# Dense gates of an encoder layer: part of one plane moves from VectorE to ScalarE, in four small instructions per eight tokens

## The chip, the cores and the metric

One core of one Trainium2 chip runs the whole kernel in one launch. TensorE (PE) multiplies matrices, VectorE (DVE) and ScalarE (ACT) do element-wise work, GpSimd (POOL) issues gathers, SyncE (SP) issues most other transfers. Each engine works through its own list of instructions in order; engines wait for one another by counting semaphores. The metric is the device time of one execution in microseconds (us). Before the change three runs gave 3988.33 us as the median, from 3973.1 to 3989.22.

## The reference, cut to what matters

The kernel computes one encoder layer for 1280 tokens: a token mixer (gated linear attention, a Fourier branch, gates), a layer norm, a mixture of 16384 experts of rank one (PEER), and a last norm. The part around the change is the expert mixture. For each token and each of 8 heads the 16 best pairs of keys are taken, so a token has 128 chosen experts with 128 softmax weights:

```python
s_top, i_top = lax.top_k(s, PEER_TOPK)                       # per head, two lists of 128 keys
cand = s_top[:, :, 0, :, None] + s_top[:, :, 1, None, :]
cand_idx = i_top[:, :, 0, :, None] * PEER_NKEYS + i_top[:, :, 1, None, :]
best, pos = lax.top_k(cand.reshape(t, PEER_HEADS, -1), PEER_TOPK)
idx = jnp.take_along_axis(cand_idx.reshape(t, PEER_HEADS, -1), pos, axis=-1)
g = jax.nn.softmax(best, axis=-1).reshape(t, PEER_HEADS * PEER_TOPK)
u = peer_u[idx]
a = jax.nn.gelu(jnp.einsum('td,ted->te', xb, u), approximate=False)
out = jnp.einsum('te,ted->td', g * a, peer_v[idx])
```

For 512 of the tokens the kernel gathers the rows of the chosen experts. For the other 768 it multiplies by all experts and needs, for each token, a table of 128 x 128 gates: entry (j, i) is the sum of the weights g of those of the token's 128 slots whose expert is 128 i + j. That table is what the stage "dense gates" makes.

## The kernel before

The stages follow one another, with a barrier of all engines between them: projection, attention, Fourier branch, merge, norm, best keys, best pairs, dense gates, experts. Only the function `dense_gates` (L1714 on) is changed.

Its 128 partitions are a token's 128 slots. On partition p, `R.i` and `R.j` hold for every token the two key numbers of the slot's expert, and `R.g_hi`, `R.g_lo` the slot's weight in two parts of 16 bits; `R.i`, `R.g_hi` and `R.g_lo` hold each value twice (TWICE = 2). VectorE works on eight tokens at a time (an octet, OCT = 8), in four instructions over 1024 elements of 16 bits per partition:

- L1780 compares the numbers 0 to 127 with the token's i: `hot_i`, one-hot over i (layout 64 pairs x 8 tokens x 2).
- L1783 does the same with j: `hot_j`, 128 x 8.
- L1786 multiplies `hot_i` by `g_hi`: `hot_g[:, s, 0]`, the plane of high parts.
- L1787 multiplies `hot_i` by `g_lo`: `hot_g[:, s, 1]`, the plane of low parts.

`hot_j` and `hot_g` have a ring of four octets (RING, s is the place in it); `hot_i` has one buffer. For each token TensorE multiplies `hot_j` (the weights that it loads) by the token's columns of the two planes, L1802 and L1803, and sums both in PSUM. Four tokens fill a bank (a quad); four banks are in use. ScalarE copies each quad to `out` (L1816, 512 elements), and SyncE stores half a body, 32 tokens, at a time (L1760, 2 MB). A body is 64 tokens: 8 octets, 16 quads. There are 12 bodies: the first is written out, eleven run in a loop.

What sets the order: TensorE waits at an octet's first quad for `hot_ok`, which VectorE raises with L1787, and for the bank four quads back to be copied out (`ev`). ScalarE waits for each quad (`mm`), and at every eighth quad for the store that last used that half of `out` (`stored`). VectorE waits before `hot_j` for TensorE to be done with the ring place of four octets ago (`mm`), before L1786 for its own `hot_i` (`i_ok`), and at the end of each octet for its own `hot_ok`, since the next octet overwrites `hot_i`. The stage ends when the last store has landed; only then do the expert stage's first loads start.

Of the kernel before, what the change touches and what calls it, by code (L numbers as in the profile page):

```python
# [25 lines left out]
f32 = mybir.dt.float32  # L26
f16 = mybir.dt.float16
u32 = mybir.dt.uint32
ALU = mybir.AluOpType
ACT = mybir.ActivationFunctionType  # L30
AX = mybir.AxisListType

P = 128
# [11 lines left out]
PH, NKEYS, TOPK, HALF = 8, 128, 16, 128  # L45
# [6 lines left out]
ND = DT * P  # L52
# [9 lines left out]
TWICE = 2  # L62
# [1640 lines left out]
I_GROUP = 4  # L1703
# [11 lines left out]
def dense_gates(nc, A, R):  # L1715

    with ExitStack() as c:
        sb = lambda n, s, d: c.enter_context(nc.sbuf_tensor(n, s, d))  # L1720
        sem = R.semaphore
        OCT, RING, HALF_T, QUAD = 8, 4, 32, 4
        PAIRED = NKEYS // TWICE
        BODY = 2 * HALF_T
        row = sb("g_row", [P, NKEYS], f32)
        iota, iota_2 = sb("g_iota", [P, NKEYS, OCT], f16), sb("g_iota_2", [P, PAIRED, OCT, TWICE], f16)
        hot_i, hot_j = sb("g_hot_i", [P, PAIRED, OCT, TWICE], f16), sb("g_hot_j", [P, RING, NKEYS, OCT], f16)
        hot_g = sb("g_hot_g", [P, RING, 2, PAIRED, OCT, TWICE], f16)
        out = sb("g_out", [P, 2, N_GROUPS, HALF_T, I_GROUP], f32)
        ps = c.enter_context(nc.psum_tensor("g_ps", [P, 4, QUAD, NKEYS], f32))  # L1730
        iota_ok, i_ok, hot_ok, mm, ev = [sem("g_" + n) for n in "iota_ok i_ok hot_ok mm ev".split()]
        stored = [sem("g_stored0"), sem("g_stored1")]
        h_in = sem("g_h_in")
        consts, consts_all = R.consts, R.consts_in + 16
        R.consts_in = consts_all
        block = c.enter_context(nc.Block())
        NQ, NO = BODY // QUAD, BODY // OCT
        TURNS = 1
        LOOP = (ND // BODY - 1) // TURNS
        REST = [n for n in range(1 + LOOP * TURNS, ND // BODY)]  # L1740

        def bodies(eng, body):
            body(0, 0, True)
            with eng.Fori(0, LOOP) as i:
                for r in range(TURNS):
                    body(1 + TURNS * i + r, 1 + r, False)
            for n in REST:
                body(n, n, False)

        @block.sync  # L1750
        def _(sp):
            sp.dma_start(row[:], A["iota"].rearrange("(a n) -> a n", a=1).to_broadcast([P, NKEYS])).then_inc(consts, 16)
            for tile in range(GT):
                sp.dma_start(h_rows(R, tile), R.h_dram[tile].rearrange("p (k c) -> p k c", k=KO)).then_inc(h_in, 16)

            with sp.Fori(0, ND // BODY) as i:
                for h in range(2):
                    sp.wait_ge(ev, NQ * i + NQ // 2 * (h + 1))
                    dst = R.g_dram[:, :, bass.ds(BODY * i + HALF_T * h, HALF_T)].rearrange("g j t f -> j g (t f)")
                    sp.dma_start(dst, out[:, h].rearrange("p g t f -> p g (t f)")).then_inc(stored[h], 16)  # L1760
            for h in range(2):
                sp.wait_ge(stored[h], 16 * (ND // BODY))
            sp.wait_ge(h_in, 16 * GT)

        @block.vector
        def _(dve):
            dve.wait_ge(consts, consts_all)
            for t in range(OCT):
                dve.tensor_copy(iota_2[:, :, t], row[:].rearrange("p (n c) -> p n c", c=TWICE))
            dve.tensor_copy(iota[:], row[:].rearrange("p (n a) -> p n a", a=1).to_broadcast([P, NKEYS, OCT])  # L1770
                            ).then_inc(iota_ok, 1)
            dve.wait_ge(iota_ok, 1)

            def body(n, turn, first):
                for o in range(NO):
                    s = (NO * turn + o) % RING
                    toks = bass.ds(BODY * n + OCT * o, OCT)
                    each = lambda ap: ap.rearrange("p (a t) c -> p a (t c)", a=1).to_broadcast([P, PAIRED, OCT * TWICE])
                    flat = lambda ap: ap.rearrange("p n t c -> p n (t c)")
                    dve.tensor_tensor(flat(hot_i[:]), flat(iota_2[:]), each(R.i[:, toks]), ALU.is_equal).then_inc(i_ok, 1)  # L1780
                    if not first or o >= RING:
                        dve.wait_ge(mm, 2 * (NO * n + o - RING + 1))
                    dve.tensor_tensor(hot_j[:, s], iota[:], R.j[:, toks].rearrange("p (a t) -> p a t", a=1).to_broadcast(  # L1783
                        [P, NKEYS, OCT]), ALU.is_equal)
                    dve.wait_ge(i_ok, NO * n + o + 1)
                    dve.tensor_tensor(flat(hot_g[:, s, 0]), flat(hot_i[:]), each(R.g_hi[:, toks]), ALU.mult)  # L1786
                    dve.tensor_tensor(flat(hot_g[:, s, 1]), flat(hot_i[:]), each(R.g_lo[:, toks]), ALU.mult).then_inc(hot_ok, 1)  # L1787
                    dve.wait_ge(hot_ok, NO * n + o + 1)
            bodies(dve, body)

        @block.tensor
        def _(pe):
            def body(n, turn, first):
                for q in range(NQ):
                    o, s = q // 2, (NO * turn + q // 2) % RING
                    if not first or q >= 4:
                        pe.wait_ge(ev, NQ * n + q - 3)
                    if q % 2 == 0:
                        pe.wait_ge(hot_ok, NO * n + o + 1)
                    for u in range(QUAD):  # L1800
                        t = QUAD * (q % 2) + u
                        pe.matmul(ps[:, q % 4, u], hot_j[:, s, :, t], hot_g[:, s, 0, :, t], start=True, stop=False)  # L1802
                        last = pe.matmul(ps[:, q % 4, u], hot_j[:, s, :, t], hot_g[:, s, 1, :, t], start=False, stop=True)  # L1803
                    last.then_inc(mm, 1)
            bodies(pe, body)

        @block.scalar
        def _(act):
            def body(n, turn, first):
                for q in range(NQ):  # L1810
                    h = q // (NQ // 2)
                    t0 = QUAD * (q % (NQ // 2))
                    if q % (NQ // 2) == 0 and not first:
                        act.wait_ge(stored[h], 16 * n)
                    act.wait_ge(mm, NQ * n + q + 1)
                    act.activation(out[:, h, :, t0:t0 + QUAD].rearrange("p g t f -> p t g f"),  # L1816
                                   ps[:, q % 4].rearrange("p t (g f) -> p t g f", f=I_GROUP), ACT.Copy).then_inc(ev, 1)

            bodies(act, body)

# [553 lines left out]
```

## Time and profile before

| | |
|---|---|
| median of three runs | 3988.33 us |
| the profiled execution | 3981.61 us, span of its instructions 3979.9 us |
| dense gates, first octet's start to last copy's start | 1555.6 to 1814.6 us |
| in 1555 to 1815 us: PE, DVE, ACT busy | 206.39, 240.43, 114.88 of 260 us |
| granted TensorE clock there | 0.50 |

The span is counted from the first instruction to the last. In a group of instructions "128x1024 f16" is partitions by elements and the type, "x96" the number of times, and the three durations are the shortest, the median and the longest. A row of the timeline has its start in us, its duration in us, engine, line, operation, and in brackets how long the engine had stood idle before it and what ended that. An instruction's duration can overlap the next one's start on the same engine, so the time that an instruction really takes from its engine is the distance between two starts. Matmuls are pipelined and overlap each other in the same way.

### The profile page before, as it was taken

The page shows a single profiled execution, that of the slowest core. Times are in us where ns is not written, and L with a number is a line of the kernel's source. Part 1 is how long each engine was busy: PE and PEld are TensorE (multiplying, and loading weights), DVE is VectorE, ACT ScalarE, POOL GpSimd, SP SyncE. Part 2 cuts the span into 40 slices and gives each one's busy share as a digit, 9 for nine tenths or more (in the row PEclk, how much of TensorE's full clock was granted, in tenths as well). Part 3 has the DMA queues.
Part 4 walks back from the last instruction along what each step waited for, and adds up shares of the span by engine and source line. Part 5 has one row for each costly group of instructions (what it writes and reads, how often), then busy time and mean ns, then how long its engine had stood idle before and what let it go on. Part 6 is the DMA issues. An engine that isn't in the chain of part 4 may idle for free. (4 is left out here: it accounts for less than half of the span.)

```text
span 3979.9 us, 59043 instructions
## 1 busy us (share of the span) xinstructions
PE 3521.8 (88%) x19562; PEld 1975.0 (50%) x19562; DVE 3010.2 (76%) x5573; ACT 1502.1 (38%) x2654; POOL 877.8 (22%) x943
## 2 busy tenths in 40 slices
PE   7988669996899386776899999999999999999995
PEld 3556535553455244674454545454545555454542
DVE  3444235555499798995888888888988898888888
ACT  3732233443233343443333333333333333333332
POOL 1210012220011010001233323332333333333323
PEclk9986589998899697557999999999999999999998
DMA  6740157873110102667889898999989898989885
GB/s 265 286 199 14 72 223 257 281 238 138 61 42 30 67 1 69 198 197 265 341 338 360 339 353 339 352 341 352 355 337 354 338 366 330 363 337 358 341 335 190
DMA packets 284839, 996.94 MB, mean 250 GB/s; under 512 B 21008, under 2 KB 124240, under 8 KB 217552
## 3 DMA queue, kind: packets, MB, share of 16 engines
q0 software_dynamic: 110592, 671.14, 45.0%
q1 hardware_dynamic: 174160, 324.66, 22.4%
q8 instruction: 52, 0.85, 0.1%
q14 instruction: 35, 0.29, 0.0%
HBM read 860.45 MB, written 135.27 MB: 250 GB/s over the span
## 5 line engine op out<-in xcount | busy, mean ns | idle before, releaser
L1949 POOL DMA_INDIRECT x_rows<-in_peer_uv,x_index x512 | 580.6, 1134 | 1083.4 <-DVE acc L2054 946.7
L128 PE MATMUL x_ps_v<-x_v,x_w_hi 128*128 128x512 f16 x1536 | 589.6, 384 | 82.3 <-DVE acc L2060 81.3
L2054 DVE SCALAR_TENSOR_TENSOR acc<-x_rows,x_share,acc 128x1024 f32<-128x1024 f32 x512 | 656.4, 1282 | 0.0
L2190 PE MATMUL x_ps_a<-h_hi,x_u_hi 128*128 128x256 f16 (+1 forms) x2048 | 621.2, 327 | 23.2 <-ACT x_u_hi L1965 16.0
L2191 PE MATMUL x_ps_a<-h_lo,x_u_hi 128*128 128x256 f16 (+1 forms) x2048 | 620.9, 327 | 0.0
L129 PE MATMUL x_ps_v<-x_v,x_w_hi 128*128 128x512 f16 x1536 | 589.2, 384 | 0.0
L130 PE MATMUL x_ps_v<-x_v,x_w_lo 128*128 128x512 f16 x1536 | 588.5, 383 | 0.0
L1985 ACT ACTIVATE x_dots<-x_dots 128x1 f32<-128x1 f32 x512 | 103.5, 202 | 976.0 <-DVE x_dots L2078 975.9
L2078 DVE CUSTOM_DVE_ANT_0 x_rows<-h_lo,x_rows 128x1024 f32<-128x1024 f32 x256 | 312.9, 1222 | 92.3 <-DMA x_rows<-in_peer_uv,x_index 91.4
L2195 PE MATMUL x_ps_a<-h_hi,x_u_lo 128*128 128x256 f16 (+1 forms) x2048 | 374.6, 326 | 0.0
L2078 DVE CUSTOM_DVE_ANT_0 x_rows<-h_hi,x_rows 128x1024 f32<-128x1024 f32 x256 | 312.6, 1221 | 23.3 <-DMA x_rows<-in_peer_uv,x_index 22.0
L128 PEld LDWEIGHTS x_ps_v<-x_v,x_w_hi 128*128 128x128 f16 x1536 | 151.6, 99 | 277.1 <-DVE acc L2060 97.5
L2190 PEld LDWEIGHTS x_ps_a<-h_hi,x_u_hi 128*128 128x128 f16 x2048 | 201.1, 98 | 161.5 <-ACT x_u_hi L1965 16.2
L2191 PEld LDWEIGHTS x_ps_a<-h_lo,x_u_hi 128*128 128x128 f16 x2048 | 201.0, 98 | 136.4 <-issue 1.1
L2195 PEld LDWEIGHTS x_ps_a<-h_hi,x_u_lo 128*128 128x128 f16 x2048 | 200.5, 98 | 132.3
L1802 PE MATMUL g_ps<-g_hot_g,g_hot_j 128*128 128x128 f16 x768 | 195.1, 306 | 60.2 <-DVE g_hot_g L1787 60.2
L2091 DVE TENSOR_TENSOR x_w<-x_w,x_gate 128x512 f32<-128x512 f32 (+1 forms) x256 | 142.2, 555 | 135.8 <-ACT x_w L1997 134.5
L130 PEld LDWEIGHTS x_ps_v<-x_v,x_w_lo 128*128 128x128 f16 x1536 | 151.7, 99 | 185.9 <-issue 7.9
L129 PEld LDWEIGHTS x_ps_v<-x_v,x_w_hi 128*128 128x128 f16 x1536 | 151.6, 99 | 177.9 <-issue 7.0
L2060 DVE SCALAR_TENSOR_TENSOR acc<-x_ps_v,acc 128x1024 f32<-128x1024 f32 x192 | 234.2, 1220 | 0.0
L1947 POOL COPY x_index<-expert 128x4 uint32 (+1 forms) x128 | 68.9, 538 | 639.2 <-DVE acc L2054 363.2
L1974 ACT ACTIVATE x_gate<-x_gate_st 128x1024 f32<-128x1024 f32 x96 | 200.1, 2084 | 11.1 <-DMA x_gate_st<-gate_scratch 8.0
(332 smaller groups left out, 6585.4 us busy)
## 6 DMA issues: line engine op xcount, KB each, us to landing
x_u_st<-in_peer_u_t SPq DMA_DIRECT2D x128, 512.0 KB, 7.0
x_v<-v_scratch SPq DMA_DIRECT2D x128, 512.0 KB, 9.8
gate_scratch<-g_out SPq DMA_DIRECT2D x24, 2048.0 KB, 8.7
x_gate_st<-gate_scratch SPq DMA_DIRECT2D x96, 512.0 KB, 6.6
m_v_st<-in_peer_v POOLq DMA_DIRECT2D x72, 512.0 KB, 5.6
v_scratch<-m_v_out POOLq DMA_DIRECT2D x72, 512.0 KB, 4.4
p_v_st<-in_peer_v POOLq DMA_DIRECT2D x46, 512.0 KB, 8.8
v_scratch<-p_v_out POOLq DMA_DIRECT2D x46, 512.0 KB, 7.4
```

Source lines behind the costliest of these rows:

```text
L128: pe.matmul(out, lhs_hi, rhs_hi, start=first, stop=False)
L129: pe.matmul(out, lhs_hi, rhs_lo, start=False, stop=False)
L130: return pe.matmul(out, lhs_lo, rhs_hi, start=False, stop=last)
L1802: pe.matmul(ps[:, q % 4, u], hot_j[:, s, :, t], hot_g[:, s, 0, :, t], start=True, stop=False)
L1949: pool.indirect_dma_start(rows[:, m % RING], None, uv_all, bass.IndirectOffsetOnAxis(ap=index[:, tile % 2, m % PER_TILE:m % PER_TILE + 1], ...
L1974: act.activation(gate[:, :, t0:t0 + PIECE], gate_st[:].rearrange("p t e -> p e t"), ACT.Copy).then_inc(gate_ok, 1)
L2054: dve.scalar_tensor_tensor(R.acc[:, DT + tile], rows[:, r, D:2 * D], share[:, s:s + 1], R.acc[:, DT + tile], ALU.mult, ALU.add).then_inc(v ...
L2060: dve.scalar_tensor_tensor(R.acc[:, t], ps_v[:, slot], 1 / (VSCALE * GSCALE), R.acc[:, t], ALU.mult, ALU.add).then_inc(added, 1)
L2078: dve.tensor_tensor_reduce(out=rows[:, k % RING, 0:D].rearrange("p (k c) -> p k c", k=KO), in0=h_rows(R, tile), in1=rows[:, k % RING, 0:D] ...
L2190: pe.matmul(out, u_hi[:, e, ko], R.h_hi[:, ko, t], start=ko == 0, stop=False)
L2191: pe.matmul(out, u_hi[:, e, ko], R.h_lo[:, ko, t], start=False, stop=False)
L2195: last = pe.matmul(out, u_lo[:, e, ko], R.h_hi[:, ko, t], start=False, stop=ko == KO - 1)
```

## The change

For tokens 4 to 7 of each octet the plane of low parts is made by ScalarE: one Copy per token of that token's 128 columns of `hot_i`, with the slot's `g_lo` as a scale per partition (function `lows`). [...] VectorE's product with `g_lo` covers tokens 0 to 3 only. `hot_i` gets two buffers, because ScalarE reads it while VectorE goes on. A new semaphore `low_ok` says that ScalarE is done with an octet: TensorE waits for it at the octet's second quad, and VectorE before it overwrites the `hot_i` of two octets ago.

```diff
--- before.py
+++ after.py
@@ -1724,11 +1724,13 @@
         BODY = 2 * HALF_T
         row = sb("g_row", [P, NKEYS], f32)
         iota, iota_2 = sb("g_iota", [P, NKEYS, OCT], f16), sb("g_iota_2", [P, PAIRED, OCT, TWICE], f16)
-        hot_i, hot_j = sb("g_hot_i", [P, PAIRED, OCT, TWICE], f16), sb("g_hot_j", [P, RING, NKEYS, OCT], f16)
+        hot_i, hot_j = sb("g_hot_i", [P, 2, PAIRED, OCT, TWICE], f16), sb("g_hot_j", [P, RING, NKEYS, OCT], f16)
         hot_g = sb("g_hot_g", [P, RING, 2, PAIRED, OCT, TWICE], f16)
+        low = sb("g_low", [P, ND], f32)
+        HALF_O = OCT // 2
         out = sb("g_out", [P, 2, N_GROUPS, HALF_T, I_GROUP], f32)
         ps = c.enter_context(nc.psum_tensor("g_ps", [P, 4, QUAD, NKEYS], f32))
-        iota_ok, i_ok, hot_ok, mm, ev = [sem("g_" + n) for n in "iota_ok i_ok hot_ok mm ev".split()]
+        iota_ok, i_ok, low_ok, hot_ok, mm, ev = [sem("g_" + n) for n in "iota_ok i_ok low_ok hot_ok mm ev".split()]
         stored = [sem("g_stored0"), sem("g_stored1")]
         h_in = sem("g_h_in")
         consts, consts_all = R.consts, R.consts_in + 16
@@ -1768,7 +1770,8 @@
             for t in range(OCT):
                 dve.tensor_copy(iota_2[:, :, t], row[:].rearrange("p (n c) -> p n c", c=TWICE))
             dve.tensor_copy(iota[:], row[:].rearrange("p (n a) -> p n a", a=1).to_broadcast([P, NKEYS, OCT])
-                            ).then_inc(iota_ok, 1)
+                            )
+            dve.tensor_copy(low[:], R.g_lo[:, :, 0]).then_inc(iota_ok, 1)
             dve.wait_ge(iota_ok, 1)
 
             def body(n, turn, first):
@@ -1777,14 +1780,21 @@
                     toks = bass.ds(BODY * n + OCT * o, OCT)
                     each = lambda ap: ap.rearrange("p (a t) c -> p a (t c)", a=1).to_broadcast([P, PAIRED, OCT * TWICE])
                     flat = lambda ap: ap.rearrange("p n t c -> p n (t c)")
-                    dve.tensor_tensor(flat(hot_i[:]), flat(iota_2[:]), each(R.i[:, toks]), ALU.is_equal).then_inc(i_ok, 1)
+                    if not first or o >= 2:
+                        dve.wait_ge(low_ok, NO * n + o - 1)
+                    dve.tensor_tensor(flat(hot_i[:, o % 2]), flat(iota_2[:]), each(R.i[:, toks]), ALU.is_equal
+                                      ).then_inc(i_ok, 1)
                     if not first or o >= RING:
                         dve.wait_ge(mm, 2 * (NO * n + o - RING + 1))
                     dve.tensor_tensor(hot_j[:, s], iota[:], R.j[:, toks].rearrange("p (a t) -> p a t", a=1).to_broadcast(
                         [P, NKEYS, OCT]), ALU.is_equal)
                     dve.wait_ge(i_ok, NO * n + o + 1)
-                    dve.tensor_tensor(flat(hot_g[:, s, 0]), flat(hot_i[:]), each(R.g_hi[:, toks]), ALU.mult)
-                    dve.tensor_tensor(flat(hot_g[:, s, 1]), flat(hot_i[:]), each(R.g_lo[:, toks]), ALU.mult).then_inc(hot_ok, 1)
+                    dve.tensor_tensor(flat(hot_g[:, s, 0]), flat(hot_i[:, o % 2]), each(R.g_hi[:, toks]), ALU.mult)
+                    few = bass.ds(BODY * n + OCT * o, HALF_O)
+                    dve.tensor_tensor(hot_g[:, s, 1, :, 0:HALF_O].rearrange("p n t c -> p n (t c)"),
+                                      hot_i[:, o % 2, :, 0:HALF_O].rearrange("p n t c -> p n (t c)"),
+                                      R.g_lo[:, few].rearrange("p (a t) c -> p a (t c)", a=1).to_broadcast(
+                                          [P, PAIRED, HALF_O * TWICE]), ALU.mult).then_inc(hot_ok, 1)
                     dve.wait_ge(hot_ok, NO * n + o + 1)
             bodies(dve, body)
 
@@ -1797,6 +1807,8 @@
                         pe.wait_ge(ev, NQ * n + q - 3)
                     if q % 2 == 0:
                         pe.wait_ge(hot_ok, NO * n + o + 1)
+                    else:
+                        pe.wait_ge(low_ok, NO * n + o + 1)
                     for u in range(QUAD):
                         t = QUAD * (q % 2) + u
                         pe.matmul(ps[:, q % 4, u], hot_j[:, s, :, t], hot_g[:, s, 0, :, t], start=True, stop=False)
@@ -1806,15 +1818,33 @@
 
         @block.scalar
         def _(act):
+            act.wait_ge(iota_ok, 1)
+
+            def lows(n, o, s, first):
+                act.wait_ge(i_ok, NO * n + o + 1)
+                if not first or o >= RING:
+                    act.wait_ge(mm, 2 * (NO * n + o - RING + 1))
+                for t in range(HALF_O, OCT):
+                    last = act.activation(hot_g[:, s, 1, :, t], hot_i[:, o % 2, :, t], ACT.Copy,
+                                          scale=low[:, bass.ds(BODY * n + OCT * o + t, 1)])
+                last.then_inc(low_ok, 1)
+
+            def evacuate(n, q, first):
+                h, t0 = q // (NQ // 2), QUAD * (q % (NQ // 2))
+                if t0 == 0 and not first:
+                    act.wait_ge(stored[h], 16 * n)
+                act.wait_ge(mm, NQ * n + q + 1)
+                act.activation(out[:, h, :, t0:t0 + QUAD].rearrange("p g t f -> p t g f"),
+                               ps[:, q % 4].rearrange("p t (g f) -> p t g f", f=I_GROUP), ACT.Copy).then_inc(ev, 1)
+
             def body(n, turn, first):
-                for q in range(NQ):
-                    h = q // (NQ // 2)
-                    t0 = QUAD * (q % (NQ // 2))
-                    if q % (NQ // 2) == 0 and not first:
-                        act.wait_ge(stored[h], 16 * n)
-                    act.wait_ge(mm, NQ * n + q + 1)
-                    act.activation(out[:, h, :, t0:t0 + QUAD].rearrange("p g t f -> p t g f"),
-                                   ps[:, q % 4].rearrange("p t (g f) -> p t g f", f=I_GROUP), ACT.Copy).then_inc(ev, 1)
+                for o in range(NO):
+                    lows(n, o, (NO * turn + o) % RING, first)
+                    for q in (2 * o - 2, 2 * o - 1):
+                        if q >= 0:
+                            evacuate(n, q, first)
+                for q in (NQ - 2, NQ - 1):
+                    evacuate(n, q, first)
 
             bodies(act, body)
 
```

The lists of instructions show what stands where. In them a wait is named after the semaphore's first use in the program, which is another stage's name. On ScalarE before, in the loop's body: `p_w_in1` is `mm`, `p_left_out1` is `stored`.

```order
L1815 REGISTER_ALU [waits p_left_out1]
L1816 ACTIVATE g_out<-g_ps 128x4x32x4 [waits p_w_in1]
L1815 REGISTER_ALU
L1816 ACTIVATE g_out<-g_ps 128x4x32x4 [waits p_w_in1]
L1815 REGISTER_ALU
L1816 ACTIVATE g_out<-g_ps 128x4x32x4 [waits p_w_in1]
```

On ScalarE in the changed kernel, the same loop, third octet of a body: `p_x_in1` is `i_ok`, `p_left_out0` is `mm`. L1828 is the new Copy, L1837 the copy out of PSUM.

```order
L1826 ISA [waits p_x_in1]
L1828 ISA [waits p_left_out0]
L1828 ACTIVATE g_hot_g<-g_hot_i,g_low 128x64x2
L1828 ISA
L1828 ACTIVATE g_hot_g<-g_hot_i,g_low 128x64x2
L1828 ISA
L1828 ACTIVATE g_hot_g<-g_hot_i,g_low 128x64x2
L1828 ISA
L1828 ACTIVATE g_hot_g<-g_hot_i,g_low 128x64x2
L1836 REGISTER_ALU
L1837 ACTIVATE g_out<-g_ps 128x4x32x4 [waits p_left_out0]
L1836 REGISTER_ALU
```

Four Copies of octet o now stand ahead of the two copies out of octet o - 1 on the same engine, each with an instruction that computes the address of its scale. At a body's end the copies out of the last octet stand ahead of the next body's first four.

On VectorE before, one octet in the loop: `p_w_in0` is `hot_ok`.

```order
L1780 ISA [waits p_w_in0]
L1780 TENSOR_TENSOR g_hot_i<-g_iota,i 128x1024
L1782 ISA
L1783 REGISTER_ALU [waits p_w_in1]
L1783 TENSOR_TENSOR g_hot_j<-g_iota,j 128x1024
L1785 REGISTER_ALU
L1786 REGISTER_ALU [waits p_x_in1]
L1786 TENSOR_TENSOR g_hot_g<-g_hot_i,g_hi 128x1024
L1787 REGISTER_ALU
L1787 TENSOR_TENSOR g_hot_g<-g_hot_i,g_lo 128x1024
```

On VectorE in the changed kernel, one octet in the loop: `p_w_in1` is now `hot_ok`, `p_w_in0` is `low_ok`.

```order
L1785 ISA [waits p_w_in0,p_w_in1]
L1785 TENSOR_TENSOR g_hot_i<-g_iota,i 128x1024
L1788 ISA
L1789 REGISTER_ALU [waits p_left_out0]
L1789 TENSOR_TENSOR g_hot_j<-g_iota,j 128x1024
L1791 REGISTER_ALU
L1792 REGISTER_ALU [waits p_x_in1]
L1792 TENSOR_TENSOR g_hot_g<-g_hot_i,g_hi 128x1024
L1794 REGISTER_ALU
L1794 TENSOR_TENSOR g_hot_g<-g_hot_i,g_lo 128x64x8
```

The number of instructions per octet is the same; the fourth product is half as long, in runs of 8 elements, and the wait at the octet's head names two semaphores in one instruction.

## Rows read from the trace of the kernel before

**Rows 1.** Windows: busy time by engine (and count), granted clock, DMA share, GB/s.
```profile
1555.00:1815.00 260.00, 206.39 (x1536) 180.73 (x1536) 240.43 (x385) 114.88 (x192) 0.00 (x0) 0.50 0.67 191
```
**Rows 2.** Waits from 1550 to 1830 us: who for whom, us, times, longest.
```profile
ACT g_out L1816 <- PE g_ps L1803: 162.3, 192, 21.5
PE g_ps L1802 <- DVE g_hot_g L1787: 60.2, 96, 10.1
```
**Rows 3.** Timeline of VectorE: one octet, the next one's start, a loop turn.
```profile
1678.13 0.69 DVE L1780 TENSOR_TENSOR g_hot_i<-g_iota,i 128x1024 f16<-128x1024 f16 x1 [0.15 <-DVE g_hot_g L1787]
...
1679.94 0.69 DVE L1787 TENSOR_TENSOR g_hot_g<-g_hot_i,g_lo 128x1024 f16<-128x1024 f16 x1
1680.78 0.70 DVE L1780 TENSOR_TENSOR g_hot_i<-g_iota,i 128x1024 f16<-128x1024 f16 x1 [0.15 <-DVE g_hot_g L1787]
...
1662.21 0.69 DVE L1780 TENSOR_TENSOR g_hot_i<-g_iota,i 128x1024 f16<-128x1024 f16 x1 [0.45 <-DVE g_hot_g L1787]
1683.73 0.69 DVE L1780 TENSOR_TENSOR g_hot_i<-g_iota,i 128x1024 f16<-128x1024 f16 x1 [0.45 <-DVE g_hot_g L1787]
```
**Rows 4.** Timeline of TensorE and ScalarE after that octet.
```profile
1680.68 0.33 PE L1802 MATMUL g_ps<-g_hot_g,g_hot_j 128*128 128x128 f16 x1 [0.51 <-DVE g_hot_g L1787]
1680.95 0.30 PE L1802 MATMUL g_ps<-g_hot_g,g_hot_j 128*128 128x128 f16 x1
1681.90 0.60 ACT L1816 ACTIVATE g_out<-g_ps 128x512 f32<-128x512 f32 x1 [1.10 <-PE g_ps L1803]
1682.43 0.30 PE L1802 MATMUL g_ps<-g_hot_g,g_hot_j 128*128 128x128 f16 x1
1682.89 0.60 ACT L1816 ACTIVATE g_out<-g_ps 128x512 f32<-128x512 f32 x1 [0.38 <-PE g_ps L1803]
```
**Rows 5.** VectorE's groups by form: busy us, mean ns, idle before.
```profile
L1787 DVE TENSOR_TENSOR g_hot_g<-g_hot_i,g_lo 128x1024 f16<-128x1024 f16 x96 | 65.9, 687 | 0.0
L2091 DVE TENSOR_TENSOR x_w<-x_w,x_gate 128x512 f32<-128x512 f32 x128 | 88.6, 692 | 135.8 <-ACT x_w L1997 134.5
L2091 DVE TENSOR_TENSOR x_w<-x_w,x_gate 128x256 f32<-128x256 f32 x128 | 53.6, 419 | 0.0
L2054 DVE SCALAR_TENSOR_TENSOR acc<-x_rows,x_share,acc 128x1024 f32<-128x1024 f32 x512 | 656.4, 1282 | 0.0
```
**Rows 6.** ScalarE's groups by form, same columns.
```profile
L1251 ACT ACTIVATE k_k_hi<-k_w_st 128x128 f16<-128x128 f32 x16 | 4.7, 294 | 0.0
L1985 ACT ACTIVATE x_dots<-x_dots 128x1 f32<-128x1 f32 x512 | 103.5, 202 | 976.0 <-DVE x_dots L2078 975.9
L1989 ACT ACTIVATE x_share<-x_dots,soft 128x1 f32<-128x1 f32 x512 | 150.8, 295 | 84.5 <-ACT x_dots L1985 76.2 <-issue 5.7
L1965 ACT ACTIVATE x_u_hi<-x_u_st 128x1024 f16<-128x1024 f32 x128 | 134.2, 1049 | 130.5 <-DMA x_u_st<-in_peer_u_t 130.5
L1974 ACT ACTIVATE x_gate<-x_gate_st 128x1024 f32<-128x1024 f32 x96 | 200.1, 2084 | 11.1 <-DMA x_gate_st<-gate_scratch 8.0 <-issue 3.1
```
**Rows 7.** Timeline of ScalarE where nothing ends a wait between two starts.
```profile
666.90 0.46 ACT L960 ACTIVATE m_s<-m_ps,m_b_mg 128x256 f32<-128x256 f32 x1
667.26 0.47 ACT L962 ACTIVATE m_s<-m_ps,m_b_mg 128x256 f32<-128x256 f32 x1
...
1390.45 0.38 ACT L1515 ACTIVATE g_hi<-b_ps 128x256 f16<-128x256 f32 x1 [4.34 <-PE b_ps L1697]
1390.73 0.38 ACT L1516 ACTIVATE i<-b_ps 128x256 f16<-128x256 f32 x1
```
**Rows 8.** Timeline: VectorE's start, the stage's end, DMA issues (size, us to landing).
```profile
1554.85 0.69 DVE L1770 CAST g_iota<-g_row 128x1024 f16<-128x1024 f32 x1
1555.57 0.69 DVE L1780 TENSOR_TENSOR g_hot_i<-g_iota,i 128x1024 f16<-128x1024 f16 x1
1824.95 0.84 SPq L1887 DMA_DIRECT2D x_u_st<-in_peer_u_t  x2
...
gate_scratch<-g_out SPq DMA_DIRECT2D x24, 2048.0 KB, 8.7
```

## The prediction

> **What bounds the kernel now.** I read the windows first, over the stage of the dense gates, 1555 to 1815 us: VectorE is busy 240.43 of 260 us, TensorE 206.39, ScalarE 114.88, at a granted clock of 0.50, which is TensorE's 1.2 GHz level [rows 1]. So VectorE is nearly full and ScalarE is not half so. Then the waits of that stretch: TensorE waits for VectorE's last product at each of 96 octets, 60.2 us in all; ScalarE waits for TensorE at each of 192 quads, 162.3 us in all [rows 2]. Nobody is named that VectorE waits for. The reader is to see a chain with VectorE at its head.
>
> The timeline gives its pace. Three starts of VectorE lie (1679.94 - 1678.13) / 3 = 0.603 us apart; from the fourth to the next octet's first, behind VectorE's wait for its own result, there are 0.84 us: 2.65 us per octet [rows 3]. One turn of the loop, eight octets, takes 1683.73 - 1662.21 = 21.52 us, 0.32 us more than 8 x 2.65. Twelve bodies are 258.2 us. TensorE starts its matmuls (1682.43 - 1680.95) / 12 = 0.123 us apart, so an octet's 16 need 1.97 us, and the second quad's copy starts 2.21 us after the first matmul [rows 4]. The expert stage's first load is issued at 1824.95 us, after the last store, and nothing of it starts before [rows 8]: what this stage loses or wins reaches the end of the kernel whole.
>
> **The change part by part.** *VectorE's fourth product is halved.* The trace has no product of 512 16-bit elements. It has the products over 1024 at 687 ns, and products of 32-bit elements at 692 ns for 512 and 419 ns for 256 [rows 5]. The 16-bit product of 1024 costs what a 32-bit one of 512 costs, so two elements pass per step; 512 of them then cost 419 ns if that rate holds, 692 ns if it falls to one per step. It now runs in pieces of 8 elements instead of 16 with a jump between; L1783 already has one operand in repeated pieces of 8 and keeps its 0.60 us of pace [rows 3]. I take 419: it goes with the rate of this very instruction. That removes 687 - 419 = 0.268 us per octet, all on VectorE's chain: 2.65 becomes 2.38, and 96 x 0.268 = 25.7 us.
>
> *Four Copies on ScalarE.* 128 elements with a scale written into the instruction take 294 ns; a scale read from a table adds 295 - 202 = 93 ns (L1989 against L1985) [rows 6]: 0.387 us. Where nothing is waited for, the next start comes before the end: 0.36 us after a start of 0.46 us, 0.28 after 0.38 [rows 7], so 0.10 us overlaps. A Copy takes 0.29 us of ScalarE, a copy out of PSUM 0.60 - 0.10 = 0.50: 4 x 0.29 + 2 x 0.50 = 2.16 us per octet, against 2.38 that VectorE leaves. The cover is ScalarE's own idle time: 162.3 us before [rows 2], 25.7 less because the stage is shorter, less 96 x 1.16 = 111.4, leaves 25. Price on the path: nothing, while the sum stays under 2.38. The address of each scale is computed by an instruction between the Copies; in the merge stage two ACTIVATEs with a scalar operand follow each other at 0.36 us [rows 7], and I expect the same with the address instruction, since it can run while the Copy before it is under way. If it can't, that is the case without overlap below.
>
> *Who is late next.* Counted from an octet's first VectorE start, `hot_i` is there at 0.69 us, the Copies run from about 0.83 to 2.1, `hot_ok` comes at 2.23, TensorE's second quad at 2.23 + 0.05 + 8 x 0.123 = 3.26: `low_ok` is early by over a microsecond. At a body's end the order is worse: the copies of the last two quads stand ahead of the next body's first four Copies. The last quad is ready at 4.49 us, the copy holds ScalarE to 4.99, the Copies end near 6.4, and TensorE's second quad of the new octet, due at 5.96, waits some 0.4 us. TensorE has 2.38 - 1.97 = 0.41 us to spare per octet and catches up in the next. VectorE needs that `low_ok` only at the third octet of the body, at 7.5 us. So this costs nothing, by 1.1 us.
>
> *VectorE's new wait.* It stands in one instruction with the old one. Behind it in VectorE's list is the whole octet, and TensorE waits for that. L2054 waits for two semaphores in the expert stage and shows 0.0 us of idle over 512 instructions [rows 5]; the other end is a wake-up per octet, 1680.68 - 1680.63 = 0.05 us from VectorE's end to TensorE's start [rows 3, 4], 4.8 us in all. I take 1 us, near the first, whose wait is likewise over when it is reached.
>
> *The table `low`*, 768 elements: the cast of 1024 took 1555.57 - 1554.85 = 0.72 us [rows 8]. Between 0.4 (half the elements at the same rate) and 1.0 (one element per step, by the 32-bit products). I take 0.7, once.
>
> *The stores.* 24 of 2 MB, 8.7 us each to landing [rows 8]. Half a body takes 10.8 us now and 9.7 then. ScalarE needs a half of `out` back only when the other half has been filled, so 8.7 us still fits, and two stores don't overlap.
>
> *Sum:* -25.7 + 0.7 + 1.0 = -24.0 us. Against the profiled execution's 3981.6 us that is 3957.6; the median of the three runs stands 6.7 us above it, so the forecast is 3988.3 - 24.0 = **3964 us**.
>
> Two rules of the Trainium skill speak to this. The first speaks against the change: "ScalarE: Activation LUTs", section "Rules for kernel authors", gives multiplications to VectorE, which is up to about three times as fast per element in 16 bits. The prices above agree: ScalarE's four Copies are 1.16 us for what VectorE did in 0.268; the sum by the rule's engine time alone would be +0.9 us per octet, the sum by the waits is -0.268, and as long as ScalarE stands idle the second decides. The other is in "Advanced Engine Details and Errata", section "SBUF Cachelines": an access wants at least two hits in a line of 16 bytes, and each new line otherwise costs. Here a Copy reads and writes pairs of 4 bytes, 32 bytes apart: two hits, so by the rule no price, but at its limit; L1974, with one hit of 4 bytes per 16, took 2084 ns [rows 6]. That the rule holds with exactly two hits no row here shows.
>
> **The rivals.**
> *A. ScalarE's Copies don't overlap.* Every one waits for its address. Then 4 x 0.387 + 2 x 0.50 = 2.55 us per octet, over 2.38: ScalarE is the bound, and 96 x 2.55 = 244.8 us stand against 258.2: -13.4 + 0.7, **3976 us**. If the copies out of PSUM don't overlap either, 2.75 us, 263.8 us, 3995. For it: the Copies are the shortest in a row of this stage, and no row has four in a row with an address between. Against: rows 7.
> *B. The other side: the pairs are slow on ScalarE.* L1974 reads one 32-bit element per 16 bytes and takes 2084 ns where L1965 takes 1049 for as many [rows 6], 1.01 ns more per element. If a Copy pays that on its 128 elements, it takes 0.29 + 0.13 = 0.42 us. With the copies out of PSUM at their full 0.60, since each waits for TensorE, an octet is 4 x 0.42 + 1.20 = 2.88 us: 276 us against 258.2, and with the table **4007 us**, slower. With overlap everywhere 2.68 us, about 3988; with none anywhere 3.26 us, 4044. It decides where ScalarE's sum passes 21.52 / 8 = 2.69 us. For it: L1974. Against: a pair is not a single element, and L1816 writes pieces of 16 bytes at 0.60 us.
> *C. The half product is no faster*, since its pieces cost it the double rate: 692 ns again, no gain, +0.7 + 1: **3990 us**. For it: no row has this shape. Against: L1783.
> *D. TensorE or the stores take over.* 1.97 us and 8.7 us are under the new pace; the least likely.
>
> **How the numbers follow.** Forecast 0.60, A 0.15, C 0.10, B 0.12, D or another 0.03. The forecast's own range is 3956 to 3972: from the bounds of the wait and the cast, and a few us of spread between runs. The whole range is 3955 to 3996: it takes in A, C and B's mild end, and leaves out B's price and a little below, under 2 in 10. Half a per cent, about what a measurement of this kernel can tell from no change, is 20 us: below 3968.4 or above 4008.3. The forecast lies below that line in four of five of its cases (0.48), and A in a few (0.01): faster 0.49. Slower is half of B and what is left, 0.08. The rest, 0.43, is within.
>
> **What would show it.** In the changed profile: VectorE's fourth product at about 419 ns (692 shows C), its start-to-start 2.38 us per octet and some 19.4 us per turn; no idle time of VectorE put down to a Copy of ScalarE, except perhaps near a body's start. The new Copies at 0.39 us each and 0.29 us apart: 0.39 apart is A, 0.5 long is B. ScalarE still waiting for TensorE or VectorE, some 25 us in all. The stage some 24 us shorter and the expert stage unchanged. It is wrong if VectorE waits for `low_ok` in every octet, or if the stage shrinks and the rest grows.

## The result: half a per cent faster

The changed kernel takes 3961.5 us, the median of 7 runs (3949.49 to 3965.95), against 3981.89 us of the kernel before, also 7 runs (3970.14 to 3989.22). The ratio is 0.9949 with a 95% interval of 0.9934 to 0.9965, some 20 us less. Five later runs of it beside eleven of the kernel before gave 0.9938 (0.9926 to 0.9951), 22.7 us less. The forecast's step was -24.0 us, and its 3964 us lies 2.5 us above the median. That this is so near is in part luck: the three runs that it started from have a median 6.4 us above that of all seven, and its step was 3.6 us larger than the one these runs show, so the two errors cancel in part.

In the profile the stage of the dense gates is to be read, from VectorE's first cast of the table `g_iota` to the issue of the expert stage's first load. Its start before, then its start and end now (the end before is in [rows 8]):

```profile
1553.76 1.18 DVE L1769 CAST g_iota<-g_row 128x128 f16<-128x128 f32 x8 [5.43 <-DMA g_row<-in_iota]
```
```profile
1565.15 1.18 DVE L1771 CAST g_iota<-g_row 128x128 f16<-128x128 f32 x8 [5.45 <-DMA g_row<-in_iota]
...
1813.16 0.84 SPq L1917 DMA_DIRECT2D x_u_st<-in_peer_u_t  x2
```

Before, that was 1553.76 to 1824.95 us, 271.2 us; now it is 248.0 us. So the stage is 23.2 us shorter. The span of the profiled execution is only 3979.9 - 3961.6 = 18.3 us shorter, because its unchanged part ahead of the stage took 11.4 us more and the part behind it some 6.5 us less. Over the profiles of this study, whose code is the same outside this stage, the first part ends between 1552 and 1566 us and the last takes 2137 to 2159 us, so such differences come without any change there.

The windows of the changed kernel (us from and to, length, busy us of TensorE, its weight load, VectorE, ScalarE and GpSimd with counts, granted clock, DMA share, GB/s):

```profile
1555.00:1795.00 240.00, 202.54 (x1517) 177.06 (x1518) 214.28 (x391) 213.84 (x558) 2.35 (x1) 0.71 0.71 202
```

ScalarE was busy 114.88 of 260 us [rows 1]; now it is as busy as VectorE. The groups by form between 1550 and 1820 us and the waits between 1550 and 1810 us:

```profile
L1794 DVE TENSOR_TENSOR g_hot_g<-g_hot_i,g_lo 128x512 f16<-128x512 f16 x96 | 40.1, 418 | 0.0
...
L1828 ACT ACTIVATE g_hot_g<-g_hot_i,g_low 128x128 f16<-128x128 f16 x384 | 126.9, 408 | 24.5 <-DVE g_hot_i L1785 19.8
...
L1837 ACT ACTIVATE g_out<-g_ps 128x512 f32<-128x512 f32 x192 | 103.7, 584 | 8.3 <-PE g_ps L1815 8.3
```
```profile
ACT g_out L1837 <- PE g_ps L1815: 8.3, 24, 0.5
...
PE g_ps L1814 <- DVE g_hot_g L1794: 33.4, 78, 10.3
...
DVE g_hot_i L1785 <- DVE g_hot_g L1794: 12.9, 79, 0.6
DVE g_hot_i L1785 <- ACT g_hot_g L1828: 5.8, 9, 0.7
...
PE g_ps L1814 <- ACT g_hot_g L1828: 2.8, 11, 0.5
```

The fourth product takes 418 ns for 687 before [rows 5]. ScalarE's wait for TensorE has gone from 162.3 us [rows 2] to 8.3. The 19.8 us at L1828 are something else: 18.9 of them are one wait, before the first octet. No wait of ScalarE for a store is in the list. Two waits of VectorE stand at L1785, the start of an octet: one for its own last result, one for ScalarE's Copies. The timeline of VectorE shows where they lie (start, us, engine, line, operation, idle time before it and what ended that):

```profile
1566.24 0.68 DVE L1772 CAST g_iota<-g_row 128x1024 f16<-128x1024 f32 x1
1566.84 0.55 DVE L1774 CAST g_low<-g_lo 128x768 f32<-128x768 f16 x1
1567.42 0.69 DVE L1785 TENSOR_TENSOR g_hot_i<-g_iota,i 128x1024 f16<-128x1024 f16 x1
...
1661.33 0.69 DVE L1785 TENSOR_TENSOR g_hot_i<-g_iota,i 128x1024 f16<-128x1024 f16 x1 [0.15 <-DVE g_hot_g L1794]
...
1663.14 0.42 DVE L1794 TENSOR_TENSOR g_hot_g<-g_hot_i,g_lo 128x512 f16<-128x512 f16 x1
...
1664.20 0.69 DVE L1785 TENSOR_TENSOR g_hot_i<-g_iota,i 128x1024 f16<-128x1024 f16 x1 [0.64 <-ACT g_hot_g L1828]
...
1666.59 0.69 DVE L1785 TENSOR_TENSOR g_hot_i<-g_iota,i 128x1024 f16<-128x1024 f16 x1 [0.15 <-DVE g_hot_g L1794]
...
1683.79 0.69 DVE L1785 TENSOR_TENSOR g_hot_i<-g_iota,i 128x1024 f16<-128x1024 f16 x1 [0.64 <-ACT g_hot_g L1828]
```

An octet is 1666.59 - 1664.20 = 2.39 us, for 2.65 before. A turn of eight is 1683.79 - 1664.20 = 19.59 us, for 21.52 [rows 3]. Inside the turn VectorE waits 0.15 us per octet for its own last product, as before; at the turn the idle time is 0.64 us instead of 0.45, and the row names a Copy. ScalarE and TensorE around the turn at 1664.20 us:

```profile
1662.24 1.33 ACT L1828 ACTIVATE g_hot_g<-g_hot_i,g_low 128x128 f16<-128x128 f16 x4
1663.46 1.07 ACT L1837 ACTIVATE g_out<-g_ps 128x512 f32<-128x512 f32 x2
...
1665.79 0.60 ACT L1837 ACTIVATE g_out<-g_ps 128x512 f32<-128x512 f32 x1 [0.38 <-PE g_ps L1815]
1666.40 2.55 ACT L1828 ACTIVATE g_hot_g<-g_hot_i,g_low 128x128 f16<-128x128 f16 x8
...
1667.88 0.29 PE L1814 MATMUL g_ps<-g_hot_g,g_hot_j 128*128 128x128 f16 x1 [0.22 <-ACT g_hot_g L1828]
```

Four Copies take 1.33 us and each 0.41, so they start (1.33 - 0.41) / 3 = 0.31 us apart. At a body's end the last two copies out of PSUM stand ahead of the next Copies; eight of these then follow in a row, and TensorE waits 0.22 us for the first four.

### The profile page after: what moved, and what is told of

It reads as the page before. It is cut to its first block, busy times and chain, and to the rows that moved or that the text cites. A ratio compares the mean times of both kernels' runs of the same rounds, so it can differ in the third digit from the quotient of the medians.

```text
span 3961.6 us, 60149 instructions
## 1 busy us (share of the span) xinstructions
PE 3529.8 (89%) x19562; PEld 1984.1 (50%) x19562; DVE 2984.3 (75%) x5574; ACT 1607.7 (41%) x3038; POOL 881.1 (22%) x943
## 4 chain that ended last, share of the span: by engine, by line
PE 22%; DMA 13%; DVE 13%; issue 5%; ACT 1%; DVEq 0%; POOLq 0%; POOL 0%; SPq 0%; ACTq 0%
DMA x_rows<-in_peer_uv,x_index 12%; DVE acc L2084 6%; PE x_ps_a L2225 4%; PE x_ps_a L2220 4%; PE x_ps_a L2221 4%; PE x_ps_v L128 3%; PE x_ps_v L129 3%; PE x_ps_v L130 3%; DVE x_rows L2108 3%; DVE acc L2090 1%; DVE x_w L2121 1%; DVE x_w_lo L2127 1%; DMA x_gate_st<-gate_scratch 1%; ACT x_w L2027 0%; DVE x_stats L2177 0%
```

## The experiments

All are edits of the changed kernel, shown cut to the lines that matter. Where the text says one run, the time is that of a single execution, and the stage is what is to be read. The question is what of the 23 us belongs to the moved work. The theory is the prediction's: VectorE is the bound, and its octet became shorter by half a product. The rivals that the profile leaves: the wait for VectorE's own result can be had without moving anything; and ScalarE, nearly full, is a second bound close by.

**Only the wait is moved.** ScalarE makes nothing, VectorE the whole fourth product. The second buffer of `hot_i`, which the change brought along, is used to let VectorE wait for an octet's results only two octets later.

```diff
-        HALF_O = OCT // 2
+        HALF_O = OCT
-                        dve.wait_ge(low_ok, NO * n + o - 1)
+                        dve.wait_ge(hot_ok, NO * n + o - 1)
-                    dve.wait_ge(hot_ok, NO * n + o + 1)
```

> The kernel before with two buffers for the plane of i, and VectorE's wait at the head of an octet moved back: it waits for its products of two octets ago, no longer for those it has just issued. ScalarE makes no part of the plane. The stage runs from the first cast to the expert stage's first load: 271.2 us before, 248.0 after the change. Theory (VectorE's own chain, 2.65 us per octet, is the pace, and 0.24 us of it is the wait for its own last product): 2.41 us per octet, stage 271.2 - 96 x 0.235 = 248.6 us, as short as the change itself made it, with ScalarE as idle as before. Rival (VectorE needs that time anyway, to finish a product before the next; only less work helps): stage 271 us.

3956.14 us, ratio 0.9942 (0.9919 to 0.9965); the stage takes 245.7 us. VectorE's timeline, two octets and the start of the next turn:

```profile
1679.97 0.69 DVE L1784 TENSOR_TENSOR g_hot_i<-g_iota,i 128x1024 f16<-128x1024 f16 x1
...
1682.38 0.69 DVE L1784 TENSOR_TENSOR g_hot_i<-g_iota,i 128x1024 f16<-128x1024 f16 x1
...
1699.24 0.69 DVE L1784 TENSOR_TENSOR g_hot_i<-g_iota,i 128x1024 f16<-128x1024 f16 x1
```

An octet is 2.41 us, four products 0.60 apart and nothing between them. The turn is 1699.24 - 1679.97 = 19.27 us = 8 x 2.41: its stall is gone as well. The wait, shown as 0.15 us of idle, cost 2.65 - 2.41 = 0.24 us per octet, since without it the next product starts before the last one's end. With the turn's stall gone too, the stage is 25.5 us shorter than before. Moving this wait gains as much as the change does, with no work moved.

**Wait and work both moved**, with three tokens of eight on ScalarE (`HALF_O = 5`) and with four as in the change:

```diff
                         dve.wait_ge(low_ok, NO * n + o - 1)
+                        dve.wait_ge(hot_ok, NO * n + o - 1)
-                    dve.wait_ge(hot_ok, NO * n + o + 1)
```

> The changed kernel with the wait moved back as in the kernel with the late wait alone, and ScalarE making three tokens of eight. Theory (pace is the larger of two sums: VectorE 2.65 - 0.235 - 3 x 0.067 = 2.21 us, ScalarE 3 x 0.31 + 1.06 = 1.99 us per octet): 2.21 us, stage about 230 us, 18 shorter than after the change, and some 41 shorter than before: about 0.990 of the time before. Rival (TensorE, 16 matmuls of 0.122 us plus a wait per quad, or the stores, 24 of 8.7 us, take over): no shorter than 2.3 us per octet, stage 238 us or more, with VectorE idle for TensorE's mm.

> As before this one in the list, but with four tokens on ScalarE as in the change. Theory: VectorE's sum is 2.15 us, ScalarE's 4 x 0.31 + 1.06 = 2.29 us per octet, so ScalarE is the bound: stage about 237 us, some 7 longer than with three tokens although VectorE has less to do, VectorE idle for ScalarE's low_ok in most octets. Rival (only VectorE's work counts): 2.15 us, stage 224 us, shorter than with three tokens.

Three tokens: 3933.87 us, ratio 0.9894 (0.9863 to 0.9924), stage 227.0 us. Four: 3927.58 us, 0.9887 (0.986 to 0.9915), stage 226.5 us, where 237 were expected. The windows of the first, then those of the second, 1600 to 1750 us:

```profile
1600.00:1750.00 150.00, 143.68 (x1093) 129.00 (x1091) 150.00 (x272) 137.57 (x342) 0.00 (x0) 0.82 0.83 237
```
```profile
1600.00:1750.00 150.00, 139.46 (x1092) 130.38 (x1090) 146.31 (x273) 149.96 (x409) 0.00 (x0) 0.89 0.82 235
```

With three tokens VectorE has no idle time left and ScalarE has 12 us; with four ScalarE has none and VectorE 3.7 us. VectorE's timeline with four, the third octet of two bodies that follow each other:

```profile
1682.13 0.69 DVE L1786 TENSOR_TENSOR g_hot_i<-g_iota,i 128x1024 f16<-128x1024 f16 x1 [0.40 <-ACT g_hot_g L1828]
...
1699.78 0.69 DVE L1786 TENSOR_TENSOR g_hot_i<-g_iota,i 128x1024 f16<-128x1024 f16 x1 [0.43 <-ACT g_hot_g L1828]
```

A turn is 17.65 us, 2.21 per octet. VectorE's own octet is 2.14. It waits once per turn, not in most octets as the theory had it: at a body's third octet, which needs the Copies of the first, and these stand behind the copies out of the body before. ScalarE never stops, so 2.21 is what ScalarE needs, where the theory had put 2.29. The two bounds meet between three tokens and four, and the two versions can't be told apart. A third limit is near: a store takes 8.7 us to landing [rows 8], and half a body now takes 17.65 / 2 = 8.8.

**Five tokens on ScalarE**, with VectorE's wait as in the change. TensorE then waits for the Copies at an octet's first quad already.

```diff
-        HALF_O = OCT // 2
+        HALF_O = 3
-                    else:
                         pe.wait_ge(low_ok, NO * n + o + 1)
```

> The changed kernel, wait as it is, with five tokens of eight on ScalarE. Theory: VectorE 2.32 us, ScalarE 5 x 0.31 + 1.06 = 2.60 us per octet: ScalarE is the bound, stage about 266 us, most of the gain gone; VectorE's idle time before its first product is put down to ScalarE's Copy in nearly every octet. Rival (the gain comes from VectorE's shorter product alone, ScalarE is never late): 2.32 us, stage 241 us.

3975.73 us, ratio 0.9994 (0.9977 to 1.0011), stage 270.3 us: the gain is gone. The wait that matters between 1570 and 1800 us, and VectorE's timeline at a body's third octet:

```profile
DVE g_hot_i L1785 <- ACT g_hot_g L1827: 37.7, 45, 2.2
```
```profile
1688.33 0.69 DVE L1785 TENSOR_TENSOR g_hot_i<-g_iota,i 128x1024 f16<-128x1024 f16 x1 [2.20 <-ACT g_hot_g L1827]
```

VectorE now waits for ScalarE, 2.2 us in one go where the copies of the last two quads stand ahead of the next Copies. To see that it is this order, the last two copies of a body were put behind the first Copies of the next, still with five tokens:

```diff
-                for q in (NQ - 2, NQ - 1):
-                    evacuate(n, q, first)
+                        elif not first:
+                            evacuate(n - 1, NQ + q, False)
             bodies(act, body)
+            for q in (NQ - 2, NQ - 1):
+                evacuate(ND // BODY - 1, q, False)
```

> The kernel with five tokens on ScalarE, with the two copies out of a body's last octet moved behind the next body's first Copies, as within a body. Theory (five tokens lose twice: ScalarE's sum of 2.48 us per octet is the pace, and at each body's end its order makes VectorE stand for 2.2 us): the long stop goes, stage 270.4 - 11 x 1.6 = about 253 us, pace 2.48 us throughout. Rival (the order at a body's end is of no account, the sum alone makes 270): stage stays within 3 us of 270.

One run: 3969.67 us beside 3982.05 of the kernel before, stage 253.4 us, 17 less. The longest wait of VectorE for a Copy is 0.7 us instead of 2.2, and the window of 1600 to 1750 us shows ScalarE without a pause:

```profile
DVE g_hot_i L1785 <- ACT g_hot_g L1827: 23.7, 63, 0.7
```
```profile
1600.00:1750.00 150.00, 128.40 (x964) 113.14 (x962) 130.40 (x242) 150.00 (x424) 0.00 (x0) 0.51 0.74 211
```

So the order at a body's end was worth 17 us of the five tokens' loss; the 5.4 us left, 253.4 against 248.0, go with the 63 short waits for a ScalarE that is now the bound.

**Single elements instead of pairs.** The Copies read 16-bit elements 16 bytes apart (from `iota`) and write as before, so the low parts of these tokens aren't the real ones.

```diff
-  last = act.activation(hot_g[:, s, 1, :, t], hot_i[:, o % 2, :, t], ACT.Copy,
+  last = act.activation(hot_g[:, s, 1, :, t], iota[:, :, t].rearrange("p (n c) -> p n c", c=TWICE), ACT.Copy,
```

> The changed kernel, but ScalarE's Copies read single 16-bit elements 16 bytes apart (a column of the table iota) in place of the token's pairs of hot_i, which leaves out the true low parts of tokens 4 to 7. Theory (ScalarE's price goes by how many elements it takes from a piece; pairs at 32 bytes are free, singles are not): Copies of about 0.41 + 0.13 = 0.54 us, ScalarE's sum 4 x 0.44 + 0.96 = 2.7 us per octet, over VectorE's 2.38: stage 275 us or more, VectorE idle for ScalarE's Copy, the gain gone. Rival (128 elements cost the same however they lie): Copies of 0.41 us, stage 248 us as after the change.

One run: 3978.83 us beside 3982.05, stage 270.3 us, where 275 or more were expected. The groups:

```profile
L1828 ACT ACTIVATE g_hot_g<-g_iota,g_low 128x128 f16<-128x128 f16 x384 | 172.8, 538 | 19.2 <-DVE g_hot_i L1785 19.2
...
L1785 DVE TENSOR_TENSOR g_hot_i<-g_iota,i 128x1024 f16<-128x1024 f16 x96 | 66.5, 692 | 39.3 <-ACT g_hot_g L1828 33.3 <-DVE g_hot_g L1794 5.7
```

A Copy takes 538 ns instead of 408, and VectorE waits for it 33.3 us. This is rival B's mechanism, and it costs the whole gain; the pairs don't show it.

**Four buffers for `hot_i`**, so that VectorE needs the Copies of four octets ago, not two. If the 0.64 us at the turn is late Copies, it goes.

```diff
-        hot_i, hot_j = sb("g_hot_i", [P, 2, PAIRED, OCT, TWICE], f16), sb("g_hot_j", [P, RING, NKEYS, OCT], f16)
+        hot_i, hot_j = sb("g_hot_i", [P, 4, PAIRED, OCT, TWICE], f16), sb("g_hot_j", [P, RING, NKEYS, OCT], f16)
-                    if not first or o >= 2:
-                        dve.wait_ge(low_ok, NO * n + o - 1)
+                    if not first or o >= 4:
+                        dve.wait_ge(low_ok, NO * n + o - 3)
```

> The changed kernel with four buffers for the plane of i, so that VectorE waits for ScalarE's Copies of four octets ago in place of two. Theory (VectorE's 0.64 us at each turn of the loop, 0.19 more than before the change, is the path of instructions behind its own wait, and only put down to ScalarE because a Copy happens to end then): 0.64 us stays, stage 248 us. Rival (the Copies are late there): the turn falls back to 0.45 us, stage about 246 us.

One run: 3970.84 us beside 3982.05, stage 249.8 us. The stall at the turn stays as it was, so the Copy named beside it isn't its cause. The next two octets now wait longer too, 0.24 us for 0.15:

```profile
1685.27 0.69 DVE L1785 TENSOR_TENSOR g_hot_i<-g_iota,i 128x1024 f16<-128x1024 f16 x1 [0.64 <-ACT g_hot_g L1828]
...
1687.74 0.69 DVE L1785 TENSOR_TENSOR g_hot_i<-g_iota,i 128x1024 f16<-128x1024 f16 x1 [0.24 <-DVE g_hot_g L1794]
...
1690.21 0.69 DVE L1785 TENSOR_TENSOR g_hot_i<-g_iota,i 128x1024 f16<-128x1024 f16 x1 [0.24 <-ACT g_hot_g L1828]
```

The trace also counts the register instructions with which VectorE's list computes and waits (marked q; the number of times, then shortest, median and longest in ns). Before the change, after it, and with four buffers:

```profile
L1780 DVEq FUSED_REGOPS  x77: 69/69/82, 1578.6 to 1809.8; - x77
```
```profile
L1785 DVEq FUSED_REGOPS  x88: 69/69/82, 1585.8 to 1798.2; - x88
```
```profile
L1784 DVEq ALU_OP  x22: 40/40/40, 1588.8 to 1788.7; - x22
```

The loop turns eleven times, so the change put one more such instruction into each turn. It stands at the turn and carries the wait for the Copies: there the two waits of an octet's head are two instructions, where the list of one octet shows one. Four buffers put in two more per turn, ahead of just those two octets, which start 0.09 us later for it; 22 times that is 1.9 us, and this stage is 1.8 us longer than the change's. So here an added wait cost VectorE an instruction's time even where what it waits for was long done. At the turn that is about half of the 0.19 us by which the stall has grown. The other half lies between the loop's branch and the next instruction, 0.29 us from start to start for 0.19 before, and its cause stays open.

**TensorE's operands put together**, first the weights alone, then both. In both, the matmuls read contiguous elements that aren't the right tokens', and in the second both matmuls of a token read the plane of high parts. The operands alone are shown:

```diff
-  hot_j[:, s, :, t]
+  hot_j[:, s, 16 * t:16 * t + 16].rearrange("p n t -> p (n t)")
```
```diff
-  hot_g[:, s, 0, :, t]
+  hot_g[:, s, 0, 8 * t:8 * t + 8].rearrange("p n t c -> p (n t c)")
```

> The changed kernel with TensorE loading as weights 128 elements that lie together, in place of a token's column of hot_j, 16 bytes from one to the next; this leaves out the right result of the matmuls. Matmuls start 0.122 us apart after the change, at granted clocks of 0.5 and of 1.0 alike. Theory (the weights' load, 0.146 us each, sets that pace): load and pace fall, toward 0.06 us where the clock is 1.0; the stage stays at 248 us, since VectorE is the pace. Rival (the moving pairs, 32 bytes apart, set it): pace stays at 0.12 us.

> The changed kernel with both of TensorE's operands read from 128 elements that lie together (weights and moving), which leaves out the right result of the matmuls. Theory (after the weights alone changed the pace by 0.004 us only, the moving pairs set it): matmuls well under 0.12 us apart, about 0.06 where the granted clock is 1.0. Rival (a load of weights and a short matmul that follow each other have this pace however their operands lie): still about 0.118 us.

Weights alone, one run: 3960.97 us beside 3982.05, stage 247.8 us; matmuls start 0.118 us apart for 0.122. Both, one run: 3949.12 us beside 3980.83 (the median of eleven), stage 247.6 us. TensorE's timeline of the second, at a high and at a low granted clock:

```profile
1691.55 0.22 PE L1815 MATMUL g_ps<-g_hot_g,g_hot_j 128*128 128x128 f16 x1
1691.61 0.22 PE L1814 MATMUL g_ps<-g_hot_g,g_hot_j 128*128 128x128 f16 x1
...
1694.61 0.31 PE L1815 MATMUL g_ps<-g_hot_g,g_hot_j 128*128 128x128 f16 x1
1694.72 0.31 PE L1814 MATMUL g_ps<-g_hot_g,g_hot_j 128*128 128x128 f16 x1
```

The matmuls start 0.056 and 0.107 us apart, yet the stage is as long as the change's: TensorE isn't its bound, which speaks against rival D. The theory that the weights set TensorE's pace fell. The second edit differs from the first in the moving operand, and the pace fell with it; the moving operand alone, with the weights as they were, wasn't run.

**The change and the best version again**, five and six runs beside eleven of the kernel before.

> The changed kernel as it is, once more, beside the next. Theory (the whole change in time is the dense gates' stage, 23.2 us shorter; the stages before and behind it are the same code and only spread from run to run): stage 248 us again within 1 us, the time before it and behind it anywhere among those of the other runs (1552 to 1566 us before, 2140 to 2155 behind), ratio to before near 0.994. Rival (the change makes the stages behind it shorter too, since they took 6.5 us less in its first profile): the part behind it stays below that of the kernel before, 2155 us, by some 6 us.

> The kernel with the late wait and four tokens on ScalarE once more, beside the change: stage 226 us, ratio to before near 0.989, clear of the change's interval.

The change: 3958.18 us against 3980.83, ratio 0.9938 (0.9926 to 0.9951), stage 247.9 us. The part behind the stage took 2147.4 us, again below the 2155.0 of the kernel before, as the rival had asked. But the kernel before has one profile only, and the medians, 20.4 and 22.7 us less, leave nothing to gain beside the stage's 23.2. With the late wait and four tokens: 3927.59 us, 0.9877 (0.9856 to 0.9897), stage 226.1 us. This version beats both kernels, the change by some 31 us. Of these 22 lie in the stage; the rest falls in stretches whose code is the same, and why stays open.

## Why the prediction was right, step by step

- *VectorE is the bound.* Shown from three sides: its octet fell by half a product and the stage with it; it fell as much when only VectorE's wait was taken off its path; and a faster TensorE changed nothing.
- *The halved product, -25.7 us.* 418 ns for 419 forecast; (687 - 418) x 96 = 25.8 us. Rival C is out.
- *The table, +0.7 us.* From the big cast to the first octet 1567.42 - 1566.24 = 1.18 us, for 0.72 before [rows 8]: +0.46. Its lower bound took half the elements; 768 of 1024 are three quarters, at the same rate 0.54 us, and the cast of `low` took 1567.42 - 1566.84 = 0.58.
- *The new wait, +1 us.* Within a turn nothing, as taken: the octets are 2.39 us. At the turn 0.19 us more, 2.0 us over the eleven turns (the first has less). The size was off by one microsecond, since the step took both waits for one instruction. The stall isn't a late Copy: about half of what was added is the instruction that carries the second wait at the loop's head, as the run with four buffers shows; the other half stays open. Where VectorE no longer waits for its own last result, the whole stall is gone.
- *The sum, -24.0 us.* -25.8 + 0.5 + 2.0 = -23.3, and the stage lost 23.2 in the profile.
- *Copies of 0.39 us, 0.29 apart.* 0.41 and 0.31. The address instruction between them doesn't break the overlap, so rival A is out. ScalarE's sum, 2.16 us forecast, is 2.21. Rival B priced a single element, and the experiment with single elements shows that price, 0.13 us per Copy as forecast; pairs pay no more than some 0.02, if the forecast's 0.39 is right for elements that lie together; such a Copy wasn't run.
- *TensorE waits 0.4 us at a body's start.* 2.8 us at eleven turns, 0.25 each, and VectorE isn't reached by it. With five tokens the same order reached it, at the third octet of a body, where the prediction had placed VectorE's need.
- *ScalarE keeps some 25 us idle.* The rows seem to agree, 24.5 + 8.3, but the step was wrong: the 162.3 us that it started from held one wait of 21.5 us before the first quad [rows 2], which is no cover for anything. Without it 4 us were forecast, and 24.5 + 8.3 - 18.9 = 13.9 are there. This didn't matter for four tokens; with five it did.

What the prediction missed is not a step of its sum. It wrote that nobody is named that VectorE waits for, but the waits of the kernel before (1550 to 1830 us) name VectorE itself:

```profile
DVE g_hot_i L1780 <- DVE g_hot_g L1787: 16.7, 88, 0.5
```

It read in [rows 3] that 0.84 us pass from the fourth product to the next octet where 0.60 pass between products, and carried the 0.24 along. They were worth as much as the half product that it priced, and could be had with the buffer that the change adds.

On the two rules that the prediction weighed: the Trainium skill, "Advanced Engine Details and Errata", section "SBUF Cachelines", asks for two hits in a line of 16 bytes. The runs agree as far as they go: these Copies take 408 ns with two hits and 538 with one. That two are wholly free no run here shows. The Trainium skill's advice to multiply on VectorE ("ScalarE: Activation LUTs", section "Rules for kernel authors") is right on engine time: 1.24 us on ScalarE for 0.27 on VectorE, 4.6 times, where the Trainium skill has up to about three per element. The runs show where it stops deciding: with ScalarE idle the work was free at four tokens of eight, and at five, in the change's order, it cost the whole gain.

## What to carry to other kernels

Before work is moved off the engine that bounds, read what that engine waits for by itself: a wait for its own last result right before the next piece cost more here than the idle time that the profile shows, and a second buffer let it wait a piece later for free. When work is moved to an idle engine, add up both engines' time per unit, leave out the waits that lie before the first unit, and follow the order at the loop's end, where a full engine falls behind first. The two measures here nearly add up, 23.2 and 25.5 us apart and 44.7 us together, and end where both engines are full.

## What the runs showed of the hardware that was not expected

The granted clock in the stage rose with the change, 0.50 before [rows 1] and 0.71 after, and the matmuls gained nothing from it. Two stretches of the changed kernel, one at the 1.2 GHz level, one at 2.4 GHz:

```profile
1669.00:1671.00 2.00, 2.00 (x17) 1.75 (x16) 2.00 (x4) 2.00 (x6) 0.00 (x0) 0.50 1.02 290
1720.00:1722.00 2.00, 2.00 (x16) 1.83 (x16) 1.94 (x4) 1.92 (x6) 0.00 (x0) 1.00 1.02 291
```

In both TensorE runs without a break, and 16 or 17 matmuls fall into 2 us, 0.12 us each. Over the whole stage the median distance of two starts is 0.122 us at the low level and 0.123 at the high one. Only with both operands contiguous does the clock show: 0.107 us at the low level and 0.056 at the high one. So while the moving elements lie in pairs 32 bytes apart, the matmuls go at one pace whatever the clock; that it is the moving operand rests on the weights alone having changed 0.122 only to 0.118.
